# One stage instead of a row of Blocks: the recurrent branch, the latent attention and their output projection in a single program block, with edits to the dilated attention, the feed-forwards and the S5 tables

## The reference, cut to what matters

```python
def hybrid_rglru_mla(h, ...):
    proj = h @ w_in
    x_r, gate_r, c_q, c_kv, k_pe = jnp.split(proj, HY_SPLITS, axis=-1)    # 1024, 1024, 512, 256, 64
    y_a = rglru_branch(x_r, gate_r, ...)
    y_b = mla_branch(c_q, c_kv, k_pe, cos, sin, q_norm, w_uq, kv_norm, w_ukv)
    return jnp.concatenate([y_a, y_b], axis=-1) @ w_out

def rglru_branch(x_r, gate_r, ...):                                        # 8 blocks of 128
    xc = causal_depthwise_conv(x_r, conv_w) + conv_b                       # 4 taps
    r = sigmoid(xb @ gate_a_w + gate_a_b); i = sigmoid(xb @ gate_x_w + gate_x_b)   # xb: xc by blocks
    log_a = -RG_C * r * softplus(-lam)
    b = sqrt(-expm1(2.0 * log_a)) * (i * xc)
    h = scan over the tokens of (exp(log_a), b)
    return h * gelu(gate_r)

def mla_branch(c_q, c_kv, k_pe, ...):                                      # 8 heads
    q = rms_norm_2(c_q, q_norm) @ w_uq                                     # per head 128 + 64 (rotated)
    kv = rms_norm_2(c_kv, kv_norm) @ w_ukv                                 # per head 128 keys, 128 values
    return causal attention over two blocks of 128 queries, the 64 rotated columns of k_pe shared
```

## Time and profile before

| | |
|---|---|
| median of 3 runs | 2829.34 us (2827.18 to 2829.8) |
| the profiled execution | 2828.71 us |
| its span (first to last instruction) | 2826.70 us |
| mean granted TensorE clock | 0.935 of full speed |
| PE, DVE, ACT, POOL busy in the span | 90%, 57%, 43%, 21% |

### The profile page before, as it was taken

One profiled execution on the slowest core, in us unless ns is written; L12 is line 12 of the kernel. 1 busy time (PEld: TensorE's weight loads), 2 busy tenths in 40 slices (PEclk: granted clock), 3 DMA queues, 4 the chain that ended last, 5 costly groups with the idle time before them and its releaser, 6 DMA issues. The chain is left out here.

```text
span 2826.7 us, 49496 instructions
## 1 busy us (share of the span) xinstructions
PE 2553.9 (90%) x19386; PEld 2437.1 (86%) x19386; DVE 1614.9 (57%) x2742; ACT 1202.6 (43%) x1908; POOL 604.6 (21%) x434
## 2 busy tenths in 40 slices
PE   7989798999999998998999974789997999978998
PEld 6989688899888887998899974488997999978997
DVE  3769695566415444666466675346666655525665
ACT  2534464444434444444244452234444445423443
POOL 1110494000563433000000022000002556430000
PEclk9999699999999999999999996589998999988999
DMA  4465101455453332454155441033552112103452
GB/s 158 163 193 181 53 1 61 149 178 193 132 175 101 109 101 90 150 184 156 60 180 185 167 131 67 25 113 119 184 186 66 64 68 75 68 31 120 156 178 97
DMA packets 107150, 344.25 MB, mean 122 GB/s; under 512 B 20432, under 2 KB 26160, under 8 KB 106480
## 3 DMA queue, kind: packets, MB, share of 16 engines
q1 hardware_dynamic: 106992, 342.07, 37.0%
HBM read 340.86 MB, written 1.16 MB: 121 GB/s over the span
## 5 line engine op out<-in xcount | busy, mean ns | idle before, releaser
L134 PE MATMUL ps<-h_high,hi 128*128 128x256 f32 x3192 | 932.3, 292 | 48.9 <-DVE h_low L272 44.0
L135 PE MATMUL ps<-h_low,hi 128*128 128x256 f32 x3192 | 916.0, 287 | 0.0
L136 PE MATMUL ps<-h_high,lo 128*128 128x256 f32 x3192 | 914.9, 287 | 0.0
L101 ACT ACTIVATE hi<-raw 128x1024 fp32r<-128x1024 f32 x623 | 644.5, 1051 | 423.9 <-PE ps L136 409.1
L111 DVE TENSOR_TENSOR lo<-raw,hi 128x1024 fp32r<-128x1024 f32 x489 | 590.2, 1225 | 279.0 <-ACT hi L101 278.3
L134 PEld LDWEIGHTS ps<-h_high,hi 128*128 128x128 f32 x3192 | 625.7, 196 | 57.0 <-DVE h_low L272 47.2
L135 PEld LDWEIGHTS ps<-h_low,hi 128*128 128x128 f32 x3192 | 626.0, 196 | 0.5
L136 PEld LDWEIGHTS ps<-h_high,lo 128*128 128x128 f32 x3192 | 625.3, 196 | 0.0
L111 POOL TENSOR_TENSOR lo<-raw,hi 128x1024 fp32r<-128x1024 f32 x134 | 320.0, 2396 | 605.3 <-ACT hi L101 605.2
L134 PE MATMUL ps<-hidden_h,hi 128*128 128x256 f32 x1056 | 298.0, 282 | 12.1 <-DVE lo L111 11.7
L135 PE MATMUL ps<-hidden_l,hi 128*128 128x256 f32 x1056 | 299.8, 284 | 0.0
(11 more groups left out here) (447 smaller groups left out, 4120.1 us busy)
## 6 DMA issues: line engine op xcount, KB each, us to landing
raw<-in_weights SPq DMA_DIRECT2D x623, 512.0 KB, 3.5
at_bias<-bias_group SPq DMA_DIRECT2D x64, 64.0 KB, 2.8
s_bn<-in_s_bn SPq DMA_DIRECT2D x4, 512.0 KB, 5.5
consts<-in_consts SPq DMA_DIRECT2D x1, 1794.5 KB, 9.1
x<-in_x SPq DMA_DIRECT2D x1, 1024.0 KB, 4.9
s_cT<-in_s_b SPq DMA_DIRECT2D x1, 1024.0 KB, 7.6
s_cw<-in_s_c SPq DMA_DIRECT2D x1, 1024.0 KB, 9.6
s_cT<-s_rows SPq DMA_DIRECT2D x16, 64.0 KB, 4.6
```

The costliest lines, as they stand in the source:

```text
L101: act.activation(k.hi[:, item % CUT, :], k.raw[:, item % RAW, :], ACT.Copy).then_inc(k.item_rounded, 1)
L134: pe.matmul(out, wh, xh, start=start, stop=False, **more)
L135: pe.matmul(out, wh, xl, start=False, stop=False, **more)
L136: return pe.matmul(out, wl, xh, start=False, stop=stop, **more)
```

## The change

**`hybrid` is one Block of 51 items, all cut on POOL.** The order of the items is: latents (7), x (8), gate (8, with the two gate-matrix items between them), queries (6), values (2), keys (2), output (16, now by input tile, all 8 output tiles accumulating in 4 PSUM banks). The projections go through a ring of three PSUM tiles (`ring`; `freed(m)` waits for the reading of projection m-3). The items of the output projection are issued in 32 halves; beside each of the first 16 stands one attention step. The convolution, its low part, the quotient, the product with the input gate, the rotation and the scan are DVE's; POOL has the cuts and two products per tile (`ratio`, `gated`). The latents' norms are applied to the scores and values rather than to the latents.

**`attention`**: the bias matmuls of two groups take 128 columns in place of 512; projections 2 and 3 stand ahead of the wait for `a.rows`; the last key sum of a slot stands after the first item-tile of the next slot; attention steps come one projection later; the inverse of the third key norm stays in SBUF (`rt`).

**`swiglu`**: no matmuls of zeros; the first down product opens the banks (`start=opening and n % 2 == 0`), with one round of PE's loop written out.

**`S5Tables.spread_rows`**: its 17 transfers are issued by POOL after its step 3, and SP issues the weight loads without them. `make_parts` and `token_major` are gone.

```diff
@@ swiglu
-                side.fetch(sp)
-                loads(k, sp, first, 15)
-                side.spread_rows(sp)
-                loads(k, sp, first + 15, items - 15)
-            else:
-                loads(k, sp, first, items)
+                side.fetch(sp)
+            loads(k, sp, first, items)
...
-            for n in range(KT // 2):
-                pe.matmul(k.ps[:, n, :], k.zeros[:, 0:P], k.zeros[:, :], start=True, stop=False, skip_group_check=True)
...
                 for b in range(FT):
                     side.beside("gpsimd", pool, b)
+                    if b == 3:
+                        side.spread_rows(pool)
@@ S5Tables.spread_rows
-                sp.dma_start(dst, src).then_inc(self.rows.s, 16)
+                pool.dma_start(dst, src).then_inc(self.rows.s, 16)
@@ attention
                     mm.then_inc(k.item_used, 1)
+                    if g == 0 and j == 0:
+                        sums(PER - 1)
...
+            project(2)
+            sums(0)
+            project(3)
             pe.wait_ge(a.rows, 1)
...
                 if s > 1:
-                    values(q - 2)
-                    transposed(q - 1)
+                    sums(PER * s - 1)
+                    transposed(q - 2)
+                    values(q - 3)
+                    scores(q - 1)
                 beside(s, 1)
...
-                if s < HP:
-                    for i in range(3, PER):
-                        sums(PER * s + i)
+                if s < HP:
+                    sums(PER * s + 4)
@@ hybrid, TensorE
+            for m in range(2, NX):
+                project(m)
+                if m == X_AT + 1:
+                    latent_sums()
+                if m == GATE_AT - 1:
+                    swap(0)
+                if m == GATE_AT:
+                    prep.x_read(pe)
+                    gates(0)
+                if m == GATE_AT + 4:
+                    gates(1)
+            pe.wait_ge(k.low_done.s, b_low + QL + KVL)
+            for i in range(NQ):
+                queries(i)
+                if i % 2 == 0 and 2 <= i <= MH:
+                    swap(i // 2)
+            values_projected()
+            for i in range(MH):
+                keys(i)
+            scores(0)
+            scores(1)
+            pe.wait_ge(k.hy_v.s, 4)
+            for i in range(4 * KT):
+                project_out(i // 2, i % 2)
+                if i < N:
+                    transposed(i)
+                if 1 <= i <= N:
+                    values(i - 1)
+                if i + 2 < N:
+                    scores(i + 2)
@@ hybrid, VectorE
+            for n in range(KT):
+                read(X_AT + n)
+                conv(n)
+                if n:
+                    conv_low(n - 1)
...
+            def quotient(n):
+                dve.wait_ge(k.rg_tanh.s, n + 1)
+                if n >= 2:
+                    dve.wait_ge(k.rg_q.s, n - 1)
+                tick(dve.tensor_scalar(rc[:, n % 2, :], tanh[:, n, :], 1.0, None, ALU.add))
+                dve.reciprocal(rc[:, n % 2, :], rc[:, n % 2, :]).then_inc(k.rg_quotient.s, 1)
+                dve.tensor_tensor(b0[:, n, :], b0[:, n, :], xc[:, n, :], ALU.mult).then_inc(k.rg_input.s, 1)
@@ hybrid, GpSimd
+            for n in range(ITEMS):
+                cut_item(k, pool, first + n)
+                for t in {18: (0,), 19: (1, 2), 20: (3,), 23: (4,), 24: (5,), 26: (6,), 27: (7,)}.get(n, ()):
+                    ratio(t)
+                if 31 <= n < 31 + KT:
+                    gated(n - 31)
```

More of the change, by code:

```diff
@@ L508, in walk @@
             return
-        with engine.Fori(0, rounds) as i:
+        for j in range(peeled * per):
+            step(0, j)
+        with engine.Fori(peeled, rounds) as i:
             for b in range(per):
@@ L1547, in _ @@
                 if s < HP:
-                    sums(PER * s)
-                beside(s, 3)
+                    sums(PER * s + 2)
+                beside(s, 4)
                 transposed(q)
@@ L1880, in hybrid @@
     nc = k.nc
+    first = k.used
+    NX = QL + KVL + 1 + 2 * KT
+    X_AT, GATE_AT = QL + KVL + 1, QL + KVL + 1 + KT
+    Q_AT, V_AT, KN_AT, O_AT = 25, 31, 33, 35
+    ITEMS = O_AT + 2 * KT
+    GATES_AT = 16, 21
+    NQ = MH + MH // 2
+    steps = [(h, a) for h in range(MH) for a in range(2)]
+    N = len(steps)
     with ExitStack() as ctx:
@@ L1980, in _, with freed @@
             w = Weights(k, pe, first)
[L1981 to L1987 removed]
+            def freed(m):
+                if m >= 3:
+                    pe.wait_ge(k.out_done.s, b_read + m - 2)
@@ new lines, in _ @@
+            for j in range(KT):
+                prep.here(pe, j)
+                for m in range(2):
+                    mm = product(pe, ring(m), w.tile(m * ITEM + j), pair_tile(k.hp, j), start=(j == 0), stop=(j == KT - 1))
+                    if j == KT - 1:
+                        mm.then_inc(k.item_used, 1)
+            prep.sums_after(pe)
+            for m in range(2, NX):
[9 more added lines that the diff above has]
+                    gates(1)
@@ new lines, in _ @@
+            for m in range(X_AT):
+                read(m)
+                if m >= 2:
+                    latent_low(m - 2)
+            angles()
+            softplus()
+            latent_low(X_AT - 2)
+            for n in range(KT):
[3 more added lines that the diff above has]
+                    conv_low(n - 1)
+                if n == 3:
+                    inverse_columns()
+            read(GATE_AT)
+            conv_low(KT - 1)
+            read(GATE_AT + 1)
@@ L2230, in _ @@
+            for i in range(3, NQ):
+                read(NX + i)
+                if i % 2 and i <= MH + 1:
+                    rope(i // 2)
+            scan(0)
+            scan(1)
+            for n in range(4):
+                values_read(n)
+            for i in range(MH):
+                read(NX + NQ + i)
+                if i == 3:
+                    scan(2)
+            part_low(("rg", 0))
             masked(0)
-            for i in range(N):
+            scan(3)
+            for i in range(2 * MH + 2):
+                if i < N:
+                    diagonal(i)
```

900 lines of the change are left out of this document (492 added, 408 removed).

## The result

The changed kernel takes 2710.59 us, median of 4 runs (2708.43 to 2719.42), against 2828.26 us for the kernel before (4 runs). The ratio is 0.9592, 95% interval 0.9568 to 0.9615: 117.7 us or 4.1% faster. The forecast was 2711.

What follows compares the result with a forecast made beforehand. PE was taken to be at its limit in the hybrid projection, elsewhere waiting on chains of small operations, each wait also costing clock. 2828.7 - 80 - 27 - 10 - 0.7 = 2711 us, range 2670 to 2770.

Steps and rivals of the forecast that it cites:

- The hybrid layer: Nine windows, 311.4 us together, fall to 231 (191 + 24 + 5 + 11), a gain of 80.
- PE's need of 191: Hybrid layer: PE's own work at the 0.121 us matmul pitch, attention steps at 1.8 each, sums to 191 us.
- Stalls of 24 before the output: Hybrid layer: DVE and POOL hinder each other at x tiles, angles, softplus and gate quotients, 24 us of stalls together.
- Output waits of 5: Hybrid output phase: PE waits 5 us for the chain diagonal, transposed, copy, values, spread over two steps.
- The low clock, 11: Hybrid layer: eight waits above about 1.5 us, each followed by some 15 matmuls at 0.21, cost 11 us.
- Rival C: Hybrid layer: DVE and POOL serialise fully, 5.4 us per x tile, layer 266, kernel 2746 us; chance 0.28.
- Rival B: Hybrid layer: the ports hardly cost, DVE's taps slip between cuts, layer 204, kernel 2684 us; chance 0.18.
- D: First feed-forward: POOL's row loads make the kernel slower, needing 9.6 us each to eat the gain; chance 0.02.
- E: Hybrid layer: no change, as joins were hidden anyway and PE's idle 120 us return as new waits; chance 0.02.
- Dilated attention: Seven slot-end waits and slot 1's diagonal wait go, less 3 against for tail steps and `a.rows`: gain 27 us.
- S5 rows: First feed-forward: PE's 8.82 us wait for a late cut and the slow matmuls behind it go: gain 10 us.
- Zeros: Six feed-forwards: dropping the matmuls of zeros gains 0.7 us once, where the first down product doesn't wait for a cut.

Runs made afterwards that it cites:

- noread: Changed kernel with POOL writing zeros in place of the cuts of the hybrid layer's projections (31 items), matmuls kept: 2689.63 us, ratio 0.9502.
- kn8: Changed kernel whose attention output projection waits in its last slot only for the two key norms sharing its PSUM bank: 2711.18 us, ratio 0.958.
- only_hybrid: Kernel before with the new hybrid layer and its items alone; dilated attention, feed-forwards and S5 rows as before: 2751.7 us, ratio 0.9731.
- again: The changed kernel itself, unchanged, run and profiled once more as a yardstick: 2714.09 us, ratio 0.9587 to the kernel before.

## Why the prediction was right, step by step

That the total came within 1 us of 2711 is luck; the mechanism is not. From the profile before to the second one of the changed kernel the span falls by 117.1 us. The three changed stages give 80.3 (hybrid layer), 23.2 (dilated attention) and 11.7 (first feed-forward), 115.2 together. The S5 stage, in no term of the sum, gives 4.9 in this profile and took 4.0 in the first, and the rest takes 3.0.

**The hybrid layer: forecast 231 from 311.4, measured 229.4** (windows above). Here the parts held, not only the sum.

- *PE's need of 191.* The last two windows took 72.7 us for the output and the attention steps. I had 29 + 46.5 = 75.5 for them. The first two steps with their half items take 1728.05 - 1722.11 = 5.94 and later pairs 6.3, so 3.15 a step; the forecast was 3.25. The prediction's 1.8 for a step's own matmuls halves the time of the columns from the low clock to the full one; no run shows this halving. What the run shows: between 1724 and 1765 they take 1.40 and 1.82 us in turn, at a granted clock of 1.00.
- *Stalls of 24 before the output.* PE's idle times over 0.4 us from the third projection to the first output product sum to 25 in the second profile. The x tile, which I put at 4.45 between bounds of 3.0 and 5.4, took 4.65 in the mean. I had put 12 of the 24 on the x tiles and 6 on the gate phase; measured, the waits for reads of x tiles are 5.6 and those for gate tiles and a cut there 4.5, and the largest waits are at the queries and keys (3.9, 5.2 and 4.2), because DVE carries its lateness out of the x tiles and gates and PE first has the ring, then the gate tiles, to live on. The sum was right, the place partly wrong: I had looked for stalls where DVE falls behind, and they appear where PE first needs something in order.
- *Output waits of 5.* They were 0.8: one half item hides the diagonal's 1.42 entirely.
- *The low clock, 11.* From 1578.3 to 1792.3 the starts of 142 product matmuls lie some 0.21 us apart in place of 0.12, which is 13.6 us. The granted clock is 0.84 to 0.87 in three windows, each with waits of PE, 0.89 in the first and 1.00 in the others. From 1674.1 to 1677.4 it is 0.50, and in the kernel before it is 0.50 from 858 to 861, where product matmuls start 0.213 us apart, and 1.00 from 862 to 890, where they start 0.120 apart. Not every wait above 1.5 us had slow matmuls behind it, as the prediction had it: after those of 1.58, 2.37 and 2.06 us (1643.71, 1661.46, 1719.63) the matmuls start 0.12 apart at 1.00, and so they do after one of the seven slot ends in the kernel before (968.97, a wait of 1.91). With the 191 this makes 191 + 25 + 1 + 14 = 231, so the 191 was a little over 1 too high.

**Rival C, full serialisation (2746), fell by its size, not by its mechanism**: the x tiles hold eight waits for a cut, six at long taps and two at first taps, so about one per tile, as it had it. But a wait takes 1.6 to 2.0 us and not 2.44, since the cut has begun by then; the quotients mostly wait less than a cut (L2305 1.22 in the mean, 0.25 alone); and PE had the ring and the gates' items as slack, so only 25 us of stalls reached it. **Rival B (2684) fell** as a forecast, but `noread` shows the time that it described: with no cuts by POOL in the projections the hybrid layer is 199.4 by stage, 24 less; I had 27. **D** needed 9.6 us of POOL for each transfer, and it took 0.56. **E**: the steps went under the products.

**Dilated attention: forecast 27, measured 23.3 by stage.** The seven waits of 1.91 at the slot ends are gone, and slot 1 waits for nothing. What I mis-sized is the term "against", 3 us. Waits that the stage did not have before are 1.57 and 4.97 in the last slot, with the low clock behind both (0.50 from 1039.2 to 1042.5 and from 1052.8 to 1059.6), some 3 more in the opening (2.00 and 1.05 the largest) and 1.6 in the tail: 11 us. As the gain is only 4 under the forecast, something on the other side was worth more than I had; the shorter bias matmuls, to which I gave no price, may be part of it, and no run separates them. The third key norm stands last on DVE, one attention step later than before, and PE's first use of the bank waited for it although the change had taken that norm out of PSUM; `kn8` takes 3.2 to 3.5 of the 4.97 and the clock behind it back.

**S5 rows: forecast 10, measured 11.8** (12.3 by stage); the reader starts at 171.97, forecast 171.5. The size was right and the reading of its cause short: I had put the wait on the 7.70 us of issuing, and the longer part of what holds SP there is its wait of 16.1 for ACT. **Zeros: forecast 0.7, measured 0 to 0.8**, depending on the execution. The reason was right for five feed-forwards.

**Not in the prediction:** the delta net is 1.9 us longer in every profile with the new hybrid layer (462.6 against 460.7), `only_hybrid` too. Not all of it is a loss: the stretch between the two norm sums ahead of it is 1.1 shorter (18.1 against 19.2), that behind the hybrid layer 1 longer, and from the hybrid layer's end to the last norm sums it is 1.3 to 1.8 us in all. The code there is not changed, and the cause was not looked for.

## What to carry to other kernels

Where one engine's operations wait to the end of another's, as six of the 24 taps did here (2.45 to 2.51 us in place of 0.485), moving work to the idle engine costs the busy one such a wait per meeting. Price it as (how often they meet) x (what is left of the other's operation), and try shorter operations first: two halves gave back 9.6 us of the layer, where no cuts at all gave 24. A wait saved ahead of another wait is worth nothing until the second is gone too: without the zeros the wait before the first down product was 1.54 us in place of 0.68. An engine's lateness shows up not where it arises but at the next thing that is needed in order: DVE fell behind at the x tiles and gates, and PE's waits of 3.9 to 5.2 us stood at the queries and keys. A queue should not carry a transfer that waits for another engine ahead of loads that wait for nothing: on SP's that was 16.1 us against 7.70 of issuing. When an operand moves out of a shared buffer, the semaphore that guarded the buffer should move with it: here that was worth 3.2 to 3.5 us.

## What the runs showed of the hardware

What the prediction and the expectations call the port or ports stands for what makes an operation of DVE or POOL wait for one of the other; the runs show these waits and their lengths, not what lies behind them.

- **Reads from PSUM did not wait.** DVE's operation with one input in PSUM and one in SBUF took 0.416 us in the mean for the x tiles of the changed kernel, 0.421 at most, and two of the eight ran beside a cut. Its copies from PSUM (L2245) took 0.407 to 0.425, eight of the twelve beside POOL, and the rotation's products from PSUM (L2321) 0.411 to 0.419, though only one of those five met POOL.
- **The reciprocals did not wait either**: 1.753 to 1.754 us for all eight (L2306), seven of them beside POOL.
- **A tap, with two tensors in SBUF, waited out a cut**: 0.483 to 0.486 us alone, 2.45 to 2.51 when it met one. A tap that had begun before the cut kept its 0.48 (1621.00 beside the cut at 1621.33). Beside POOL's memsets, which read nothing, no tap waited: 0.483 to 0.487 over 24 taps in `noread`, ten of them beside one.
- **The other way the wait is short.** In the kernel before, the first of the two cuts of the earlier trace rows took 2.35 us; the second began 0.33 us before the end of DVE's product and took 2.53.
- **Not expected**: the first tap, a tensor-scalar whose two scalars are columns in SBUF, took 0.41 us alone, as long as the read of the tile, and up to 2.09 when it met a cut (`again`) and 1.28 when it met a memset (`noread`). The quotient's tensor-scalar (L2305), 0.25 alone in the kernel before, took 1.40 at the longest in `noread`, where it ended 0.15 us after a memset. Why these two forms waited for a memset and the taps did not was not settled.
